# Late projections of a hybrid decoder layer: the recurrence's output gate before the pool mixer's input

## The reference

```python
z = x @ p['w_in']
u_pool, hq, hf, hi, hgate, cq, ckv, kpe, gates = jnp.split(z, _split_points(), axis=-1)
y_pool, new_pool = pool_mixer(u_pool, pool_buf, pos, p['pool_w'], p['pool_scale'])   # windows 2, 4, 8, 16
o_hg, new_hg = hgrn2(hq, hf, hi, hg_state, lb)          # 4 heads, state 128 x 128 per head
o_hg = rms_norm(o_hg, p['hg_norm']) * jax.nn.silu(hgate)
# latent attention gives o_mla
merged = (g_pool * (y_pool @ p['w_br_pool']) + g_hg * (o_hg @ p['w_br_hg']) + g_mla * (o_mla @ p['w_br_mla']))
x = layer_norm(DN_ALPHA * x + merged @ p['w_out'])
x = layer_norm(DN_ALPHA * x + conv_ffn(x))
```

## Time and profile before

| | |
|---|---|
| median of 3 runs | 2555.27 us |
| profiled execution | 2558.72 us |
| its span, first to last instruction | 2556.9 us |
| TensorE busy | 2389.8 us, 93% of the span |
| VectorE busy | 1155.7 us, 45% |
| GpSimd busy | 1012.6 us, 40% |
| ScalarE busy | 529.1 us, 21% |
| mean granted TensorE clock | 0.955 of full speed |

### The profile page before, as it was taken

How to read it: one execution, slowest core, us unless ns; L and a number is a source line. 1 busy time by engine, 2 the same in 40 slices (tenths; PEclk the granted TensorE clock), 3 DMA queues, 4 the chain that set the end, 5 groups by cost and what they waited for, 6 DMA issues and landing times.

```text
span 2556.9 us, 34111 instructions
## 1 busy us (share of the span) xinstructions
PE 2389.8 (93%) x10696; PEld 1842.7 (72%) x10696; DVE 1155.7 (45%) x1783; ACT 529.1 (21%) x914; POOL 1012.6 (40%) x1248
## 2 busy tenths in 40 slices
PE   8998987999997999999899989879999979999997
PEld 6775766777775777777666757657777757777775
DVE  0633687433217666610206336874333176666002
ACT  1533211211103112100125332112111121211001
POOL 0000724467535676601200007255666266666011
PEclk9998987999998999999999989879999989999998
DMA  5221110322211221222232211103221111221222
GB/s 212 75 79 48 37 71 1 109 75 77 81 50 50 82 82 66 77 68 68 74 118 79 80 42 38 71 1 111 89 75 67 61 54 66 82 82 64 67 68 76
DMA packets 51596, 183.57 MB, mean 72 GB/s; under 512 B 7234, under 2 KB 27970, under 8 KB 37762
## 3 DMA queue, kind: packets, MB, share of 16 engines
q1 hardware_dynamic: 50882, 178.49, 20.8%
q10 hardware_dynamic: 576, 3.36, 0.3%
HBM read 172.64 MB, written 9.18 MB: 71 GB/s over the span
## 4 chain that ended last, share of the span: by engine, by line
PE 86%; DVE 7%; issue 3%; SPq 2%; ACT 1%; DMA 1%; POOL 0%; DVEq 0%; ACTq 0%; POOLq 0%
PE ps L1072 23%; PE ps L1000 19%; PE ps L1310 13%; PE ps L775 12%; PE ps L1284 5%; PE ps L1193 3%; PE ps L807 1%; DVE r L1906 1%; PE ps L993 1%; PE ps L902 1%; PE ps L828 1%; PE ps L985 1%; PE ps L816 1%; SPq L630 1%; DVE r L564 1%
## 5 line engine op out<-in xcount | busy, mean ns | idle before, releaser
L1310 PE MATMUL ps<-r,wring 128*128 128x288 f32 x1408 | 341.8, 406 | 0.0
L1310 PEld LDWEIGHTS ps<-r,wring 128*128 128x128 f32 x1408 | 267.5, 190 | 73.9
L775 PE MATMUL ps<-xT,wring 128*128 128x288 f32 (+2 forms) x1152 | 284.0, 409 | 8.4 <-DMA wring<-w_stream 6.9
L775 PEld LDWEIGHTS ps<-xT,wring 128*128 128x128 f32 x1152 | 220.4, 192 | 70.7 <-DMA wring<-w_stream 7.9
L1072 PE MATMUL ps<-lq,mreg 128*128 128x288 f32 x1056 | 263.3, 406 | 0.0
L564 POOL TENSOR_TENSOR r<-lq 128x288 f32<-128x288 f32 (+1 forms) x40 | 28.9, 722 | 538.6 <-PE ps L1221 538.6
L1072 PEld LDWEIGHTS ps<-lq,mreg 128*128 128x128 f32 x1056 | 200.6, 190 | 55.4
L1683 DVE SCALAR_TENSOR_TENSOR lq<-xT,ps 128x576 f32<-128x576 f32 x32 | 24.1, 754 | 432.5 <-PE ps L1310 319.7
L1072 PE MATMUL ps<-xT,wring 128*128 128x288 f32 x704 | 180.9, 411 | 33.3 <-ACT xT L1381 33.3
L1336 ACT ACTIVATE r<-ps 128x288 f32<-128x288 f32 (+6 forms) x240 | 103.3, 435 | 455.2 <-PE ps L1000 255.4
L1072 PEld LDWEIGHTS ps<-xT,wring 128*128 128x128 f32 x704 | 135.5, 193 | 71.9 <-issue 34.2
(11 more groups left out here) (326 smaller groups left out, 4267.4 us busy)
## 6 DMA issues: line engine op xcount, KB each, us to landing
wring<-w_stream SPq DMA_DIRECT2D x100, 1024.0 KB, 4.9
wring<-w_stream SPq DMA_DIRECT2D x32, 704.0 KB, 4.2
r<-pages_in SPq DMA_DIRECT2D x80, 128.0 KB, 2.1
vbuf<-w_stream SPq DMA_DIRECT2D x12, 512.0 KB, 3.6
r<-w_stream SPq DMA_DIRECT2D x12, 512.0 KB, 3.6
mreg<-pages_in SPq DMA_DIRECT2D x32, 128.0 KB, 2.1
r<-hgrn_state SPq DMA_DIRECT2D x2, 2048.0 KB, 8.5
hgrn_s<-r SPq DMA_DIRECT2D x2, 2048.0 KB, 6.6
```

Source lines behind the costliest of these rows:

```text
L775: mm = pe.matmul(out[0:w.shape[-1], a * 512:a * 512 + hi - lo], w, x[:, lo:hi], start=(k == 0), stop=(k == len(pairs) - 1))
L1310: mm = pe.matmul(slot(tile)[:, a * 512:a * 512 + HALF], w[k], hT[:, part * KF_HALF + k, a * HALF:(a + 1) * HALF], start=(part == 0 and k = ...
```

## The change

The four gate tiles come before the four tiles of the pool mixer's input: in the tile numbers, in TensorE's loop, in ScalarE's program and in the order of the weights in DRAM. In ScalarE's program the decays of head 1 now stand between the gate's second and third tile, and the four mixer copies are last. The programs of VectorE, GpSimd and SyncE keep their order.

```diff
-TILE_U = TILE_END_B
-TILE_HGATE = TILE_U + 4
-TILE_YPOOL = TILE_HGATE + 4
+TILE_HGATE = TILE_END_B
+TILE_U = TILE_HGATE + 4
+TILE_YPOOL = TILE_U + 4
...
-    last += [TILE_U + 1, TILE_U + 3, TILE_HGATE + 1, TILE_HGATE + 3]
+    last += [TILE_END_B + 1, TILE_END_B + 3, TILE_END_B + 5, TILE_END_B + 7]
...
-                for tile in range(TILE_U, TILE_YPOOL):
-                    j = (tile - TILE_U) % 2
-                    if tile >= TILE_U + 4:
+                for tile in range(TILE_HGATE, TILE_YPOOL):
+                    j = (tile - TILE_HGATE) % 2
+                    if tile >= TILE_U:
                         pe.wait_ge(*taken_at(l, tile - 4))
                     if j == 0:
                         pe.wait_ge(*w_ready[(n) % 2].at(l, 16 * ((n) // 2 + 1)))
-                    x_product(tile, n, j, 256 if tile < TILE_HGATE else HALF).then_inc(tile_ready.sem, 1)
+                    x_product(tile, n, j, HALF if tile < TILE_U else 256).then_inc(tile_ready.sem, 1)
...
+                def take_gate(j):
+                    act.wait_ge(*tile_ready.at(l, TILE_HGATE + j + 1))
+                    copy(two(hg_gate[:, j, :]), halves(TILE_HGATE + j), ACT.Silu).then_inc(tile_act.sem, 1)
+
+                take_gate(0)
+                take_gate(1)
+                decays_small(1)
+                decays_big(1)
+                decays_ends(1)
+                take_gate(2)
+                take_gate(3)
                 act.wait_ge(*ext_ready.at(l, 1))
                 for g in range(POOL_GROUPS):
                     act.wait_ge(*tile_ready.at(l, TILE_U + g + 1))
...
-                decays_small(1)
-                decays_big(1)
-                decays_ends(1)
-                for j in range(4):
-                    act.wait_ge(*tile_ready.at(l, TILE_HGATE + j + 1))
-                    copy(two(hg_gate[:, j, :]), halves(TILE_HGATE + j), ACT.Silu).then_inc(tile_act.sem, 1)
...
-    for w in (pool, hgate):
+    for w in (hgate, pool):
```

## The result

The changed kernel takes 2571.53 us (median of 5 runs, 2566.81 to 2575.05), the kernel before 2556.71 us beside it (5 runs, 2553.74 to 2559.68). The ratio is 1.0054, with a 95% interval of 1.0038 to 1.0071: slower by about 14 us. Forecast was slower, by 7.6 us, with 2570 us as the upper end of the range. The direction was right, the size half of what came. The kernel before stood at 2555.27 us when the forecast was made and at 2556.71 us here; 1.4 us of the distance to the forecast come from that.

What follows compares the result with a forecast made beforehand. It took unbroken TensorE projections, then the recurrence behind them, as the bound: 3.8 us a layer later, 7.6 in all, all else 0, so 2555.27 + 7.6 = 2562.9, rounded to 2563 us; range 2558 to 2570.

Steps and rivals of the forecast that it cites:

- The chain bounds what follows the last projection: Late projections and pool products: TensorE runs unbroken for 66.23 us, so only what must follow the last projection costs time.
- VectorE's group 3 behind the last copy: Last pool-mixer group: input ready 4.82 us after its start, at 336.12 us, leaving TensorE standing for 2.8 us.
- The scalings: VectorE's four scalings behind the pool groups: at most 0.82 us each, recurrence's first product 3.8 us later than 334.24.
- GpSimd's hold on VectorE: Window sums before group 3: VectorE waits until 319.6 us, yet finishes 3.3 us before group 3's input; cost 0.
- ScalarE's table loads: Decays of head 1 between gate tiles: two more loads a layer at 1.28 us, 11 us of slack, cost 0.
- SyncE's load: Sample state's load after the fourth scaling: issued some 4.1 us later, about 18 us still between, cost 0.
- The rival of a longer hold: GpSimd's series ends after 322 us, so VectorE's backlog reaches group 3: 3 us a layer, 2569 us; chance 0.07.
- The sum: Lateness of the recurrence's start: 3.8 us a layer, 7.6 us for both layers.
- the tail: VectorE's window sums and two scalings behind the last projection, delaying the recurrence; forecast at 3.8 us a layer.
- the clock falls in the new gap: Rival: TensorE's clock drops ahead of group 3's product and stays low through head 0's end: 6 us, 2569; chance 0.18.
- A sign of being wrong that came: Recurrence behind its first product: forecast wrong if its length changes by more than 2 us a layer.
- The other side: Rival: recurrence's head ends move to the upper clock, 3.3 us each; two or more moved, chance 0.06; one alone, 0.07.

Runs made afterwards that it cites:

- e3: Kernel before, old order kept, with seven additional window additions on VectorE ahead of group 3's input in each layer: 2569.29 us, +12.3 us against before.
- e2: Changed kernel with five additional matmuls on TensorE in the gap ahead of group 3's pool product: 2564.73 us, +7.7 us against the kernel before.
- e7: Kernel before with seven additional VectorE additions ahead of group 3's input and five additional TensorE matmuls in the gap: 2565.35 us, +8.3 us against before.
- e1: The changed kernel once more, unaltered, beside the kernel before: 2568.60 us, +11.6 us against before.
- e9: Changed kernel with 23 additional unread matmuls a layer on TensorE inside the recurrence: 2553.95 us, -2.7 us against the kernel before.
- e6: Kernel before with ten additional window additions on VectorE ahead of group 3's input in each layer: 2569.76 us, +12.8 us against before.
- e5: Kernel before with five additional window additions on VectorE ahead of group 3's input in each layer: 2563.07 us, +6.1 us against before.

## Why the prediction was half right

- *The chain bounds what follows the last projection.* Right. The projections take 62.34 us in either order, and the whole stretch in front of the first mask grew by what was added behind them (the gap, the scalings and the slower products).
- *VectorE's group 3 behind the last copy.* Right: forecast 4.82 us from the copy's end to the input and a gap of 2.8 us; measured 334.81 + 0.22 - 330.21 = 4.82 us and 2.83 us.
- *The scalings.* Nearly right: 3.8 us late was forecast, 3.6 measured; they overlap a little more (four in 2.99 us).
- *GpSimd's hold on VectorE, ScalarE's table loads, SyncE's load: all at nothing.* Right, by the idle times of VectorE (1.42 and 3.65 us) and by e3, where the same gap with the old order costs the same. The rival of a longer hold did not occur. GpSimd's series was even over at 315.83 us, where about 318.7 had been named as the sign, so VectorE had more slack than forecast.
- *The sum.* The term was 7.6 us; the tail is 7.2 us at the first product and 7.4 at the first mask, and where the clock is held up the kernel costs 7.7 (e2) and 8.3 (e7). This part had the right size.
- *The step that failed is the clock, set at nothing in the sum.* I had "the clock falls in the new gap" as a rival, at 6 us more and a chance of 0.18. It fell in 7 of the 8 layers of the four profiled executions with a gap of some 2.8 us and no filling there (the changed kernel, e1, e3, e9). Holding it up gives back 3.9 us, in either order (e2 against e1, e7 against e3): 7.7 + 3.9 = 11.6 us, which is e1. The first measurement, +14.8 us, holds 3 us more that no run assigns.
- *The rival's price had other terms than the cost.* It had the small products at head 0's end slowed in layer 1 and both kinds in layer 2. The small ones kept 1.95 us in both layers of the changed kernel; the four wide ones of layer 2 took 3.78 us instead of the 1.98 of the earlier trace rows. What it did not have is what comes at once, before the recurrence has begun: the last pool product (2.26 for 1.21 us) and the first scores, together 0.9 us in the changed kernel's layer 2 and 1.5 and 2.0 us in the layers of e1.
- *Why I doubted it.* The one reason against it was that the clock held through head 0's end in layer 2 of the kernel before. But the longest wait of TensorE in that stretch is 1.43 us, half the new gap, and the same wait stands in layer 1 right where the clock does fall. TensorE behind it in layer 1 and then in layer 2 of the kernel before:

```profile
348.56 0.76 PE L964 MATMUL ps<-mreg,vbuf 128*128 128x128 f32 x2 [1.43 <-DVE mreg L1912]
```

```profile
1624.04 0.49 PE L964 MATMUL ps<-mreg,vbuf 128*128 128x128 f32 x2 [1.43 <-DVE mreg L1912]
```

The same two products take 0.76 us in layer 1 and 0.49 in layer 2. The trace of the kernel before has longer waits too. At 229.76 us, in the attention for the samples, TensorE goes on after 2.20 us of waiting, and the 2 us from there on are at the lower level, where the last 2 us before the wait had 1.00:

```profile
229.76 1.97 PE L888 MATMUL ps<-const,r 128*128 128x128 f32 x8 [2.20 <-DVE r L1837]
```

```profile
229.76:231.76 2.00, 2.00 (x9) 1.69 (x9) 0.69 (x1) 0.34 (x2) 0.00 (x0) 0.50 0.03 8
```

TensorE has 15 waits of 2.20 us or more in that trace with the clock at 1.00 in the 2 us before; behind each of the 15 the granted clock of the next 2 us is below 1.00 (0.50 to 0.94). Of its 7 waits of 1.43 to 1.47 us, 4 have a lower clock behind them and 3 have not. A gap of 2.8 us was on the side of the fall, and with these rows the clock would have been a term of the sum.

- *The range.* Its upper end of 2570 us came from that rival and the one of GpSimd's longer hold, both near 2569. The changed kernel was measured at 2571.53 and at 2568.60 us, once outside the range and once inside; what both kernels scatter by from one execution to the next (6 to 8 us) deserved a wider edge.
- *A sign of being wrong that came.* The recurrence was not to change by more than 2 us a layer; it is 0.3 us longer in layer 1 and 2.3 in layer 2. In e1 the changes are -1.8 and +1.0 us, so this length varies by itself.
- *The other side,* head ends moved to the upper level by the shift: a gain from it is nowhere shown. e6 at +12.8 us, for a first mask 14.9 us late, is within its noise.

Open: what decides in one execution whether the clock falls (the changed kernel's layer 1 kept 1.00, the same kernel's in e1 did not); and what lies between the first mask's delay and the medians: 0.7, 3.1 and 2.2 us in e1, e3 and e5, 6.5 us in the first measurement. The recurrence's own length, 111 to 118 us from layer to layer without filling and with the same work, can hold it. The scatter goes with the clock: of the 61 runs of the kernel before in the experiments, the four fastest (2548.75 to 2550.51 us) had a mean granted clock of 0.959, the six slowest (2559.48 us and more) 0.955 or 0.956.

## What to carry to other kernels

Before you move independent work ahead of a producer, look at what the moved-away work was covering: here 31 us of projections hid a 5 us chain on VectorE, and the last item of that chain was the longest; with the shortest item last the same order is nearly free. Price a new gap of TensorE in front of a stretch that passes every delay on at the delay it makes, and do not set the lower clock behind it at nothing: for the gap of 2.8 us it was half as much again (3.9 us on 7.4), for gaps of 1.1 and 5.7 us these runs do not fix it. The trace that you have shows what the clock does behind waits of that length elsewhere in the kernel: look there first. Where TensorE waits for another engine on the path, try matmuls with unread results in the wait: here 23 a layer gave 18.8 us, more than the whole change cost.

## What was not expected of the hardware

- Five additional matmuls in a 2.8 us gap made the kernel 3.9 us faster; 23 in each layer's recurrence 18.8 us (0.7%), at no other change.
- The granted clock was 0.61 over 6 us around a gap of 2.83 us (e1's layer 2 and both layers of e9) and 1.00 behind gaps of 1.10 and 1.08 us (both layers of e5).
- An addition of 0.92 us on VectorE took 9.65 us under GpSimd's last series in the changed kernel, and 16.03 us with its neighbour before; GpSimd's last series shows no such stretching (an instruction on 128 x 288 elements takes 0.91 us with VectorE waiting and without). The Trainium skill, "SBUF — State Buffer", section "SBUF: two separate sides", says that whichever of the two starts first has the shared port pair for its whole instruction while the other is blocked. The wait here lasted for the series, not for one instruction.
